# One layer of the fused block: where the output projection's first four blocks are multiplied

## The reference

```
h = rms_norm(x, mix_pre_g[0])
z = h @ hy_w_in
o_a = swa_sink_attention(z's q, k, v)          # 8 heads of 64: 512 features
o_b = rwkv7_time_mix(the rest of z, ...)       # 8 heads of 64: 512 features
m = concatenate([o_a, o_b]) @ hy_w_out         # 1024 x 1024
x = x + rms_norm(m, mix_post_g[0])
x = x + rms_norm(conv_ffn(rms_norm(x, ...)), ...)
```

## Time and profile before

| | us |
|---|---|
| median of three runs (lowest, highest) | 2041.5 (2040.52, 2044.64) |
| the profiled execution: its own time | 2039.28 |
| the profiled execution: span of the trace | 2037.5 |
| mean granted TensorE clock | 0.968 of full |

### The profile page before, as it was taken

One profiled execution on the slowest core, in us unless ns is written; L12 is line 12 of the kernel. 1 busy time (PEld: TensorE's weight loads), 2 busy tenths in 40 slices (PEclk: granted clock), 3 DMA queues, 4 the chain that ended last, 5 costly groups with the idle time before them and its releaser, 6 DMA issues.

```text
span 2037.5 us, 35927 instructions
## 1 busy us (share of the span) xinstructions
PE 1887.6 (93%) x14638; PEld 1735.3 (85%) x14638; DVE 1425.1 (70%) x2154; ACT 1171.8 (58%) x2047; POOL 12.7 (1%) x25
## 2 busy tenths in 40 slices
PE   6897899989989998999899999999989997889998
PEld 6886899888769997999889867899989996868998
DVE  5676777664768777877777676877787776465555
ACT  5544656664756656655676675555565555554332
POOL 0000000020000000000000000000000000000000
PEclk9998999989989998999999999899999998989999
DMA  8302666355047664888334402688778863124551
GB/s 318 114 4 106 211 226 239 119 186 187 2 178 252 237 207 179 317 293 290 137 133 157 165 1 105 253 290 289 252 255 288 290 231 124 52 92 157 186 186 52
DMA packets 96182, 374.96 MB, mean 184 GB/s; under 512 B 5779, under 2 KB 6419, under 8 KB 95251
## 3 DMA queue, kind: packets, MB, share of 16 engines
q1 hardware_dynamic: 95376, 372.15, 51.2%
q10 hardware_dynamic: 640, 0.52, 0.1%
HBM read 371.08 MB, written 1.05 MB: 183 GB/s over the span
## 4 chain that ended last, share of the span: by engine, by line
PE 84%; DVE 9%; ACT 5%; issue 2%; DMA 0%; ACTq 0%; DVEq 0%; SPq 0%
PE psum L994 36%; PE psum L1010 17%; PE psum L696 8%; PE psum L781 5%; PE psum L977 2%; PE psum L526 2%; DVE buf L597 2%; PE psum L1612 1%; PE psum L654 1%; DVE htok L2838 1%; PE psum L2948 1%; PE psum L3396 1%; PE psum L2456 1%; DVE x_res L490 1%; DVE htok L489 1%
## 5 line engine op out<-in xcount | busy, mean ns | idle before, releaser
L994 PEld LDWEIGHTS psum<-buf,buf 128*128 128x128 f32 x6048 | 741.9, 192 | 9.3
L994 PE MATMUL psum<-buf,buf 128*128 128x256 f32 x6048 | 745.7, 283 | 0.0
L1010 PE MATMUL psum<-buf,buf 128*128 128x512 f32 x1584 | 383.6, 391 | 2.2 <-DVE buf L1059 2.2
L1010 PEld LDWEIGHTS psum<-buf,buf 128*128 128x128 f32 x1584 | 289.3, 188 | 57.8 <-DVE buf L1059 3.0
L892 DVE TENSOR_TENSOR buf<-ring,buf 128x1024 fp32r<-128x1024 f32 x264 | 311.1, 1220 | 10.0 <-DVE modT L948 7.5
L886 ACT ACTIVATE buf<-ring 128x1024 fp32r<-128x1024 f32 x264 | 262.9, 1044 | 4.1 <-DVE hT L2548 2.2
L696 PE MATMUL psum<-buf,buf 128*128 128x256 f32 x1944 | 245.9, 286 | 8.7 <-DVE buf L597 8.2
L696 PEld LDWEIGHTS psum<-buf,buf 128*128 128x128 f32 x1944 | 237.8, 193 | 14.4 <-DVE buf L597 12.9
L908 DVE TENSOR_TENSOR buf<-ring,buf 128x1024 fp32r<-128x1024 f32 x132 | 161.6, 1225 | 86.3 <-ACT buf L903 86.3
L903 ACT ACTIVATE buf<-ring 128x1024 fp32r<-128x1024 f32 x132 | 139.4, 1056 | 87.7 <-PE psum L1010 85.1
L597 DVE TENSOR_TENSOR buf<-ring,buf 128x1024 fp32r<-128x1024 f32 x97 | 118.7, 1233 | 91.9 <-ACT buf L591 84.7
(11 more groups left out here) (431 smaller groups left out, 2054.8 us busy)
## 6 DMA issues: line engine op xcount, KB each, us to landing
ring<-in_w_ffn SPq DMA_DIRECT2D x88, 1536.0 KB, 6.6
buf<-in_w_mod SPq DMA_DIRECT2D x144, 512.0 KB, 4.5
ring<-in_w_conv SPq DMA_DIRECT2D x44, 1536.0 KB, 6.5
ring<-in_w_ssd_in SPq DMA_DIRECT2D x16, 1536.0 KB, 6.5
ring<-in_w_hy_in SPq DMA_DIRECT2D x7, 1536.0 KB, 18.1
ring<-in_w_ns_in SPq DMA_DIRECT2D x7, 1536.0 KB, 7.3
ring<-in_w_ssd_out SPq DMA_DIRECT2D x5, 1536.0 KB, 6.8
ring<-in_w_cmp SPq DMA_DIRECT2D x4, 1024.0 KB, 5.1
```

The lines of the kernel that those rows point to most:

```text
L994: ins = E.matmul(b[:, g * T:(g + 1) * T], w[:, wa, g, k, :], h[:, ha, k, :], start=k + n_ == 0, stop=k == KC - 1 and n_ == 2)
L1010: ins = E.matmul(acc[:, t, g * 512:(g + 1) * 512], hr[z][:, ha, t * P:(t + 1) * P], wd[z][:, wa, g * 512:(g + 1) * 512], start=j == 0 and ...
```

## The change

`OutSteps` takes any number of homes (a home may be two separate places for high and low) and a list `turns` that gives each chunk its home; `product` may be called for one tile of tokens at a time. In `hybrid_run` there are five homes, in tiles that have fallen free: htok (q, k and v of the local attention), k and a, the level matrices, t12, and v with the tile after it. The three loads of w_hy_out keep their place in SP's queue behind the hy_in loads.

The splits of chunks 0 to 3 and of the blocks 0 to 3 of oT are moved up: w_high 0 and 1 to levels 3 and 4, w_high 2 and lhs_high 0 to 3 to level 5, w_low 0 and 1 to level 4, w_low 2 and lhs_low 0 and 1 behind the levels, lhs_low 2 between the two Q copies, w_high 3 and w_low 3 into the state's stretch, lhs_low 3 behind its first step. The products of chunks 0 to 3 stand behind the state's last product in TensorE's order: 0 (both tiles), 1, tile 0 of 2, then the transposes of tile 0, tile 1 of 2, the transposes of tile 1, and 3. The square root's table is loaded behind the copies of yc. w_high of 4 and 5 stands behind the roots; behind the last write of oT come lhs_high 4, lhs_low 4, w_low 4, and `out_project` from k = 4 on. There k = 5 has no low part yet, so it runs w_high again.

Since acc is banks 0 to 3, the state's sums that lay in bank 3 go to bank 4, its `move` from bank 4 to bank 3, and the transposes from banks 0 and 1 to banks 5 and 7. The tile sq goes to another place.

```diff
@@ -712,11 +712,13 @@
-            def __init__(self, name, n, lhs, parts_at, wp_at):
+            def __init__(self, name, n, lhs, parts_at, wp_at, turns=None):
...
                 self.parts = halves(parts_at, 4)
-                self.wp = [chunk_parts(a) for a in wp_at]
-                self.w_free, self.p_free = [[go]] * 3, [[go]] * 4
+                self.wp = [[Region(a).take(CHUNK, F32R) for a in pair] if isinstance(pair, tuple)
+                           else [chunk_parts(pair)[:, a, :] for a in range(2)] for pair in wp_at]
+                self.turns = [k % 3 for k in range(n)] if turns is None else turns
+                self.w_free, self.p_free = [[go]] * len(wp_at), [[go]] * 4
...
@@ -736,19 +738,19 @@
                     A.wait_ge(*full)
-                    for point in self.w_free[k % 3] if free is None else free:
+                    for point in self.w_free[self.turns[k]] if free is None else free:
                         A.wait_ge(*point)
-                    self.w_high_at[k] = act.count(A.activation(self.wp[k % 3][:, 0, :], raw, ACT.Copy).then_inc(act.sem, 1))
+                    self.w_high_at[k] = act.count(A.activation(self.wp[self.turns[k]][0], raw, ACT.Copy).then_inc(act.sem, 1))
...
                 s, raw, full = self.chunk(k)
-                w = self.wp[k % 3]
+                w = self.wp[self.turns[k]]
...
                     V.wait_ge(*self.w_high_at[k])
-                    self.w_at[k] = dve.count(V.tensor_tensor(w[:, 1, :], raw, whole(w[:, 0, :]), ALU.subtract).then_inc(dve.sem, 1))
+                    self.w_at[k] = dve.count(V.tensor_tensor(w[1], raw, whole(w[0]), ALU.subtract).then_inc(dve.sem, 1))
...
@@ -767,7 +769,7 @@
-            def product(self, k, after=()):
+            def product(self, k, after=(), tiles=range(NT)):
...
@@ -775,17 +777,18 @@
                     E.wait_ge(*self.w_at[k])
-                    for t in range(NT):
+                    for t in tiles:
...
                                 ins = E.matmul(acc[:, t, h * 512:(h + 1) * 512], self.parts[:, la, k % 4, t * P:(t + 1) * P],
-                                               self.wp[k % 3][:, wa, h * 512:(h + 1) * 512], start=k + n_ == 0,
+                                               self.wp[self.turns[k]][wa][:, h * 512:(h + 1) * 512], start=k + n_ == 0,
...
                                 self.done.append(p)
-                    self.w_free[k % 3] = self.p_free[k % 4] = [p]
+                    if NT - 1 in tiles:
+                        self.w_free[self.turns[k]] = self.p_free[k % 4] = [p]
...
@@ -1291,7 +1294,9 @@
             ST = [ar.take(4 * HD).rearrange("p (c i) -> p c i", c=4) for _ in range(3)]
-            t12 = Region(W_AT + 24576).take(8 * T)
+            k_at, v_at, a_at, g_at = (R_AT + 4096 * n for n in (1, 2, 5, 6))
+            t_at = W_AT + 24576
+            t12 = Region(t_at).take(8 * T)
...
@@ -1552,6 +1557,9 @@
             oT = hT
+            steps = OutSteps("w_hy_out", 8, oT, g_at, ((htok_at, htok_at + 4096), (k_at, a_at), (H_AT, H_AT + 20736),
+                                                      (t_at, H_AT + 20736 + 8192), (v_at, v_at + 4096)), (0, 1, 2, 3, 1, 0, 4, 1))
+            steps.load_to(8)
...
@@ -1671,6 +1679,8 @@
             swa_read = [(pe.sem, pe.n), (act.sem, act.n)]
+            swa_done = [(act.sem, act.n), (dve.sem, dve.n)]
+            steps.w_free[0] = [swa_read[0]]
...
@@ -1740,6 +1750,14 @@
                         t_pts.append(bank_free[o][0])
+                if l in (3, 4):
+                    steps.w_high(l - 3)
+                if l == 5:
+                    for k_ in range(2):
+                        steps.lhs_high(k_, swa_done)
+                    steps.w_high(2)
+                    for k_ in range(2, 4):
+                        steps.lhs_high(k_, [])
...
@@ -1791,6 +1809,8 @@
                             bank_free[6 + o] = [at[made]]
+                if l == 3:
+                    steps.w_free[1] = [at["gram"][1]]
...
@@ -1827,7 +1847,14 @@
                                                               scale=prm("ln_g")[:, c:c + 1]).then_inc(act.sem, 1))
+                    steps.w_low(0)
+                    steps.w_low(1)
+                    steps.w_free[2] = [at["MV", 1], lm_pts[1]]
+                    steps.p_free = [[at["bb"], at["gg"], at["gram"][1]]] * 4
             bb, gg = bon, v
+            steps.w_low(2)
+            for k_ in range(2):
+                steps.lhs_low(k_)
...
@@ -1866,13 +1893,16 @@
                     at["q", t] = dve.count(V.tensor_copy(Q[rows, t, :], bank(4 + t)[rows, :]).then_inc(dve.sem, 1))
+                if t == 0:
+                    steps.lhs_low(2)
+            steps.w_free[3] = [lm_read[1], at["Q", 1]]
...
-            H = [quarter(2, 0), quarter(3, 0), quarter(6, 0)]
+            H = [quarter(2, 0), quarter(4, 0), quarter(6, 0)]
             G = [None, quarter(7, 0), quarter(2, 1)]
-            RS = [None, quarter(3, 1), quarter(6, 1), quarter(7, 1)]
+            RS = [None, quarter(4, 1), quarter(6, 1), quarter(7, 1)]
...
@@ -1941,6 +1971,8 @@
                 at["gt", 1] = act.count(A.activation(GT[1], G[1], ACT.Copy).then_inc(act.sem, 1))
+            steps.w_high(3)
+            steps.w_low(3)
...
@@ -1967,7 +1999,7 @@
                             for o in range(2):
-                                ins = E.matmul(quarter(4, n - 1)[two[o], c, :], GT[n][two[o], c, :], ST[n - 1][two[o], c, :],
+                                ins = E.matmul(quarter(3, n - 1)[two[o], c, :], GT[n][two[o], c, :], ST[n - 1][two[o], c, :],
...
@@ -1984,7 +2016,7 @@
                                 for o in range(2):
-                                    ins = E.matmul(bank(((5, 7), (3, 6))[qt][o])[two[qb], c * HD:(c + 1) * HD],
+                                    ins = E.matmul(bank(((5, 7), (4, 6))[qt][o])[two[qb], c * HD:(c + 1) * HD],
...
@@ -1993,7 +2025,7 @@
                         V.wait_ge(*at["move"])
-                        vl(V.tensor_tensor(ST[n], ST[n], quarter(4, n - 1), ALU.add).then_inc(dve.sem, 1))
+                        vl(V.tensor_tensor(ST[n], ST[n], quarter(3, n - 1), ALU.add).then_inc(dve.sem, 1))
...
@@ -2003,9 +2035,11 @@
                                                                    ALU.add).then_inc(dve.sem, 1))
+                if n == 1:
+                    steps.lhs_low(3)
...
             sums, sq_sums = (small[:, z:z + 16].rearrange("p (t h) -> p t h", t=NT) for z in (80, 96))
-            yc, sq = (Region(W_AT + 24576 + z).take(4 * T).rearrange("p (t h i) -> p t h i", t=NT, h=8) for z in (4096, 0))
+            yc, sq = (Region(z).take(4 * T).rearrange("p (t h i) -> p t h i", t=NT, h=8) for z in (t_at + 4096, H_AT + 8192))
...
@@ -2016,6 +2050,11 @@
                     moved.append(act.count(A.activation(yc[:, t], pairs(bank(t)), ACT.Copy).then_inc(act.sem, 1)))
+            load_table(ACT.Sqrt)
+            steps.product(0, moved, [0])
+            steps.product(0, [at["S", 2]], [1])
+            steps.product(1)
+            steps.product(2, (), [0])
...
@@ -2027,7 +2066,7 @@
                             y[:, :, o, :], y[:, :, o, :],
-                            bank(((5, 7), (3, 6))[t][o])[rows, 0:T].rearrange("p (c i) -> p c i", c=4), ALU.add).then_inc(dve.sem, 1))
+                            bank(((5, 7), (4, 6))[t][o])[rows, 0:T].rearrange("p (c i) -> p c i", c=4), ALU.add).then_inc(dve.sem, 1))
...
@@ -2061,8 +2100,13 @@
                     for c in range(4):
-                        ins = E.transpose(bank(t)[:, c * P:(c + 1) * P], flat[:, c * P:(c + 1) * P], ident)
+                        ins = E.transpose(bank(5 + 2 * t)[:, c * P:(c + 1) * P], flat[:, c * P:(c + 1) * P], ident)
                     turned.append(pe.count(ins.then_inc(pe.sem, 1)))
+                if t == 0:
+                    steps.product(2, (), [1])
+            steps.product(3)
+            for k_ in (4, 5):
+                steps.w_high(k_)
...
@@ -2071,10 +2115,15 @@
                     V.wait_ge(*at["bb"])
-                    vl(V.tensor_tensor(oT[:, 4:8, tok], bank(t).rearrange("p (c n) -> p c n", c=4), gg[:, :, tok],
+                    vl(V.tensor_tensor(oT[:, 4:8, tok], bank(5 + 2 * t).rearrange("p (c n) -> p c n", c=4), gg[:, :, tok],
...
                     Ring.q = dve.count(V.tensor_tensor(oT[:, 4:8, tok], oT[:, 4:8, tok], bb[:, :, tok], ALU.add).then_inc(dve.sem, 1))
-            done = out_project(OutSteps("w_hy_out", 8, oT, *OUT_AT), [(dve.sem, dve.n), (act.sem, act.n), (pe.sem, pe.n)], nxt)
+            ready = [(dve.sem, dve.n), (act.sem, act.n), (pe.sem, pe.n)]
+            steps.w_free[4] = ready
+            steps.lhs_high(4, [Ring.q])
+            steps.lhs_low(4)
+            steps.w_low(4)
+            done = out_project(steps, ready, nxt, lambda _k: ready[0], 4)
```

## The result

| | before | changed |
|---|---|---|
| median (lowest to highest) | 2044.45 us (2040.52 to 2044.91, five runs) | 2032.91 us (2029.49 to 2035.07, five runs) |
| profiled execution, span | 2039.28, 2037.5 | 2035.07, 2033.0 |

The ratio is 0.995 with a 95% interval of 0.9938 to 0.9963, that is 7.6 to 12.7 us faster. It went the way that was forecast. The size fell short: 12.5 us were forecast, and the profiled execution, 2035.07, lies above the range, which ended at 2033; the median lies inside it by 0.1 us.

A forecast was written before the change was run, and what follows sets the result against it. TensorE, 84% of the chain, was taken as the bound. Four products off the tail 10.9, slow first product 2.15, earlier start 0.8, less a new wait of 1.3, give 12.5 us: 2041.5 to 2029.0, range 2025.8 to 2033.

The forecast's parts named there:

- part 1: Moved-up splits of chunks 0 to 3 fit into ScalarE's and VectorE's idle time; with homes and banks, taken at nothing.
- SP's queue: Next stage's second load goes at about 155, DMA engines all but idle; nothing in the queue later relative to the end.
- rival for the clock: Clock low again at product 4: 2.15 us not won, 10.3 gained, 2031.2; chance 11%.
- part 2: Square root's table load moved up from before the first root: tile 0's scaling ends some 0.6 us earlier.
- part 3: Products 0 to 3 behind the last state product, 30 matmuls taking 6.8 us; the norm gains 0.1 us only.
- part 4: Projection's last four products at full clock: product 4 starts at 182.3, product 5 at 186.3, end at 194.4.
- the loss behind the projection: Feed-forward stage waits for weights or w_mod, which come no sooner; half the gain lost gives 2035.2; chance 3%.
- The new wait: TensorE idle between products 4 and 5, 1.3 us, taken off the gain.
- The rival "Slower": Norm's transposes stand behind 30 and 36 matmuls at the slow pace of 0.406: 3.6 us slower, 2045.1; chance 3%.
- Base: Median of the kernel before, 2041.5 us, from which the forecast of 2029.0 is taken.

The follow-up runs named there:

- late_load: The changed kernel with the next stage's second weight load waiting for yc's second copy instead of w_low 2: 2029.69 us, ratio 0.9934.
- before_2: The kernel before once more, unchanged: 2040.18 us.
- late_tail_2: late_tail once more, unchanged: 2025.79 us, ratio 0.9917.
- behind: late_load with products 0 to 3 moved behind both pairs of transposes, splits, homes and banks still early: 2038.2 us, ratio 0.9981.
- turns_first: late_load with both tiles' transposes ahead of product 2: 2031.94 us, ratio 0.9948.
- late_tail: late_load with the splits of chunks 5 and 7 ahead of pre_a and pre_b, second w_high of chunk 5 dropped: 2027.38 us, ratio 0.9929.
- before_load_157: The kernel before with the next stage's first weight load, issued at 91.6, waiting for the first Q copy (157): 2041.92 us, ratio 0.9998.
- levels_load: late_load with the next stage's first weight load held back until the levels' first gram is masked (about 127): 2036.24 us, ratio 0.9959.
- after_again: The changed kernel once more, unchanged: 2032.58 us, ratio 0.995.

## Why the prediction was right in its mechanism and wrong in its sum

- **Splits, homes and banks (part 1), taken at nothing: right.** late_load's state ends at 77.3 us, before's at 77.4. The tight place before the Q copy held: 0.68 us of idle time were left in late_load, 0.4 by the forecast.
- **SP's queue, taken at nothing: the step that failed.** I wrote that the second load "goes at about 155, when the DMA engines are all but idle" and that nothing in the queue would be later. It went at 157.4. What I looked at was whether a queue was free for the load, not what else uses the DMA engines: TensorE's instructions come that way too, and this stretch eats them at 35 matmuls a microsecond, each with its weight load. Instead of nothing the step cost 4.8 to 5.2 us, by which the stretch from W to product 0 grew: a gap of 1.5 to 1.8, and about 3.3 of half clock behind it. Another 0.8 to 1.1 us of the state's later end lie in the levels, ahead of the load; before_2, late_tail_2 and behind scatter as far, and I count them to no cause. I had a rival for the clock, but placed its fall at product 4, and held against it that the gaps are 1.3 us and not 7. That was no safe reason: in the stretches of 64 x 64 matmuls gaps of 1.5, 1.8 and 2.4 us were followed by the lower level (0.50), while 1.54 us between the 512-column matmuls were not (1.00 from 190 to 198).
  The Trainium skill ("Runtime: NRT & Kernel Launch", section "Instruction fetch mechanics") says that the sequencer fetches its instructions in blocks of 16 KiB through a DMA queue of its own, and that the cost of crossing from one block to the next is mostly hidden. The trace agrees on the 16 KB packets; that the cost is hidden did not hold beside a 1.5 MB load, where it is 1.2 to 2.4 us.
- **Table load (part 2): right, and without worth here.** behind shows 0.73 us (0.6 forecast); in the changed kernel TensorE's 30 matmuls end 0.8 us later than VectorE's scaling, so it hides.
- **Products ahead (part 3): right.** From product 0's start to oT 10.9 us, forecast 10.75. The 30 matmuls took 7.0 us, 0.234 each, where I had 0.227. The Trainium skill's 0.131 us (the section cited in the prediction, "Back-to-back issue gap") did not show here either.
- **The rest of the projection (part 4): right in kind, 1.0 us too short.** Product 4 started 2.2 us behind oT, as forecast, at full clock, so the clock rival fell; and the loss behind the projection did too, since the rest is 1823.4 us against 1823.9. The new wait was 1.54 us, not 1.3: pre_a's copies started only when product 3 was done, and product 5 came 4.5 us behind product 4, forecast 4.0. The last three products took 8.5, not 8.2. That the order and not VectorE's amount of work makes this wait, turns_first and late_tail show.
- **Sums of the prediction.** The rival "Slower" is 1.0 us too slow by its own terms: from 169.4, 96 matmuls at 0.406 and 1.1 for the transposes end at 209.5, not 210.5, and oT would be written at 185.0 + 1.4 = 186.4, not 187.6. Part 3 has the first transposes done at 176.8 and goes on from 176.65. The forecast doesn't hang on either.
- **Base.** I forecast from 2041.5; seventeen runs of before gave a median of 2042.21, and two other sets of them 2041.43 and 2043.94.

In sum: 12.5 forecast, less 1.1 in the tail and 6.0 up to the state's end, makes 5.4; the first traces show 114.9 to 109.5, that is 5.4 (5.9 between the means of the three traces of before and the two of the changed kernel). With the load moved, late_load's 103.5 has 11.4 of the 12.5. That the median of 2032.91 still lies inside the range is in part luck: 5.4 off the base of 2041.5 would be 2036.1, outside it.

**What stays open.** The medians moved by 9.6 and 11.5 us, more than the 5.9 of the traces; late_load is 3 us below the changed kernel by the medians, 6 by the traces; before_load_157 is 0.9 to 2.3 us slower than the mean of before's three traces and as fast by the medians. Much of this is the 4 us that some executions lose in the second layer. The 17 executions of before fall in two groups by granted clock: eight at 0.968 with a median of 2040.3, and nine at 0.967 and below with 2044.8. All ten executions of the changed kernel are at 0.970 or 0.971 (median 2032.6), and both of its traces are without that loss. Take from each kernel the group with the higher clock (late_load from 0.972, before_load_157 from 0.968, the upper two of levels_load), and the differences between medians are 7.7 us from before to the changed kernel, 4.4 on to late_load, 1.1 for before_load_157, and 3.8 from late_load to levels_load. The traces say 5.9, 6.0, 0.9 to 2.3, and 4.3. So the stall shows outside the traces as well. But these groups were formed after the fact, and the clock moves with the change too; what is left, up to 2 us, has no cause shown. Whether the stall is a little smaller in executions without the profiler was not tested.

## What to carry to other kernels
A wait that is removed releases a load as well: for each transfer that moves, ask not only whether its data and queue are ready, but also whether an engine is then running through short instructions, tens of them in a microsecond. Put bulk loads beside long matmuls (the same 1.5 MB cost nothing beside 512-column ones) and away from runs of 64 x 64 ones. And where a step waits for a whole set of points, as pre_a for `ready`, place behind it nothing that the bound engine needs sooner.

## What the runs showed of the hardware that was not expected
- A 1.5 MB load (6.5 to 8.2 us to landing) beside a dense stretch of small matmuls stops TensorE for 1.2 to 2.4 us without a releaser: in all five traces with a load in such a stretch (changed, after_again, before_load_157 twice, levels_load), and in none of the nine without.
- Gaps of 1.5, 1.8 and 2.4 us in a stretch of 64 x 64 matmuls were followed by the lower clock, worth some 7 us at 0.50 in the first two and 3.4 in the third, though TensorE was busy all the time; gaps of 1.2 and 1.3 us were not (1.00).
- The 16 KB instruction packets follow TensorE's instructions, not time: 194 to 321 matmuls and weight loads between two of them, and 385 to 444 where such a load delayed the next.
- Executions of one kernel differ by 4 us (rest 1823.9 and 1827.9); the longer one has 10 us at a clock of 0.66 in the second layer, where the other has 1.00. Why is not shown.
